# Last three query up tiles ahead of the last key up tiles, and no projection chunks beside the first two units of the latent attention

## Chip, cores and metric

One core of one Trainium2 chip. The metric is the device time of the whole kernel in microseconds, the median of several runs. Engines: PE is TensorE (matmul; PEld its weight loads), DVE is VectorE, ACT is ScalarE, POOL is GpSimd, SP is the sync engine, on whose queue nearly all loads are issued.

## What is computed

The reference runs two blocks of two layers each on 512 tokens of width 1024. The change lies in the first block, whose two layers have this token mixer (cut to what matters):

```
proj = h @ w_in[l]
qa, ka, va, iq, ik, iw, cq, ckv, kr, ga, gb = split(proj)
ya = dsa_attention(qa, ka, va, iq, ik, iw, positions, rel_bias)     # top-128 attention
q  = rms_norm(cq) @ w_uq        # 8 heads x (64 + 32 rotary)
kv = rms_norm(ckv) @ w_ukv      # 8 heads x (64 key + 64 value)
yb = mla_attention(q_nope, rope(q_rope), k_nope, rope(kr), v)       # latent attention
merged = sigmoid(ga) * (ya @ w_branch_a) + sigmoid(gb) * (yb @ w_branch_b)
```

After it come a layer norm, a convolutional feed-forward part and a second norm. The second block (retention, differential attention) isn't touched.

## The kernel before

**Weights.** They come in slots of 128 x 2048. SP loads a slot into one of two `w_raw` buffers, ACT rounds it to `w_hi` (line 1385, `split_hi`), POOL makes the remainder `w_lo` in four parts of 512 columns (line 583). After the fourth part the semaphore `w_ready` rises and PE may use the slot. A product of weights and activations is three matmuls (`mm3`, lines 718 to 720: high by high, low by high, high by low). A chunk is one `mm3` of 128 x 128 weights on 512 columns; a tile of a projection of h has 8 chunks.

**Up tiles.** In each layer the table `UPS` gives the order of the 12 up tiles of the latent attention: 8 query tiles ("q", h), two `mm3` each, from slot `SLOT_UQ`, and 4 key tiles ("k", j), one `mm3` each, from slot `SLOT_UKV`. From position 4 on, PE adds two columns of the modulation (line 748) behind each tile. A query tile is turned by DVE (lines 2170, 2171), summed by POOL (line 620) and copied by ACT to `qm` (line 1572). A key tile is copied by ACT in two halves to `km` (lines 1578, 1579). ACT goes through `UPS` in the same order. Right behind the copy of the last query tile, q7, it rounds the next slot, `SLOT_QK`, into the buffers which the query up weights have left:

```
if j == H - 1:
    split_hi(l, SLOT_UQ + 2)
```

Four value tiles follow on PE; the third and fourth wait for banks that hold the last two tiles of `UPS`. DVE copies them to `vm` (line 2176) once the last key copy is done. ACT then rounds slot `SLOT_QK + 1`.

**Latent attention.** `attention(l, 1)` on PE goes through 32 units (4 query blocks of 128 by 8 heads; a unit of block i has i + 1 key blocks). In step t it issues the scores of unit t (S, line 831), the transposes of unit t - 2 (T, line 844), which wait for that unit's exp, the products with v of unit t - 3 (line 855), and then the chunks that `BESIDE[1][t]` lists: the 64 chunks of the query and key projections of the other attention (`SLOT_QK` to `SLOT_QK + 3`, 8 tiles). The first chunk of a slot waits for `w_ready`. From unit 2 on S waits for the logits of two units before. DVE makes the logits and their maximum (line 1952), ACT the exp (line 1461), the copy of the transposes (line 1470) and the copy of a finished projection tile (line 1454), and behind every second tile the rounding of the slot after the next. The numbers of chunks a unit are a table written by hand, 3 for units 0 to 7, 2 for 8 to 23, 1 for 24 to 31.

Both layers run this with the same tables: layer 0 reaches it at about 178 us, layer 1 at about 1015 us.

Of the kernel before, what the change touches and what calls it, by code (L numbers as in the profile page):

```python
# [28 lines left out]
H = 8  # L29
# [79 lines left out]
def build(nc, a):  # L109
    ctx = ExitStack()  # L110
    with ctx:
# [309 lines left out]
        def beside(counts, steps):  # L421
            plan = []
            for c in counts:
                plan.append(steps[:c])
                steps = steps[c:]
            return plan
# [2 lines left out]
        NI = 2 * len(PAIRS)  # L429
        gate_steps = [(t, k) for t in range(KD) for k in range(KD)]  # L430
        BESIDE = [beside([3] * H + [2] * 2 * H + [1] * H, gate_steps),
                  beside([3] * H + [2] * 2 * H + [1] * H, gate_steps),
                  beside([5, 5, 6] * 4, gate_steps)]
        BESIDE.append([[(1 + s // KD, s % KD) for s in range(4 * u, 4 * u + 4)] for u in range(14)])
        BESIDE_TILE, BESIDE_LAST = (TILE_GB, TILE_QK, TILE_GA, TILE2_G2), (KD - 1, KD - 1, KD - 1, KD - 1)
# [1 line left out]
        def ended(kind, u):  # L437
            return next((t for t, k in BESIDE[kind][u] if k == BESIDE_LAST[kind]), None) if 0 <= u < len(BESIDE[kind]) else None

        UPS = [("q", 0), ("q", 1), ("q", 2), ("k", 0), ("q", 3), ("q", 4), ("k", 1), ("q", 5), ("q", 6), ("k", 2), ("q", 7),  # L440
               ("k", 3)]
        LOADS = 16 * 3
        BIAS_UNITS = [(i, 8 * i + q) for i in range(NB) for q in range(8)]
# [266 lines left out]
        def _(pe):  # L710
            def wait_slot(l, m):
                pe.wait_ge(w_ready, slot_no(l, m) + 1)

            def wait_bank(l, t, nbanks=4):
                pe.wait_ge(tile_evac, tdone(l, t - nbanks))
# [231 lines left out]
            for l in range(DEPTH):  # L947
# [51 lines left out]
                wait_slot(l, SLOT_UQ)  # L999
                for pos, (what, j) in enumerate(UPS):  # L1000
                    wait_bank(l, TILE_UQ + pos, 2 if pos < 2 else 4)
# [369 lines left out]
        def _(act):  # L1371
# [139 lines left out]
            for l in range(DEPTH):  # L1511
# [54 lines left out]
                act.wait_ge(kr_turned, l + 1)  # L1566
                for pos, (what, j) in enumerate(UPS):
                    b = banks[pos % 4]
# [245 lines left out]
        def _(dve):  # L1814
# [294 lines left out]
            for l in range(DEPTH):  # L2109
# [54 lines left out]
                for h in range(H):  # L2164
                    pos = UPS.index(("q", h))
                    b = banks[pos % 4]
# [390 lines left out]
```

## Time and profile before

| | |
|---|---|
| median of 3 runs | 2500.24 us (2500.0 to 2502.79) |
| profiled execution, its own time | 2498.26 us |
| its span | 2496.4 us |
| granted TensorE clock, mean | 0.986 |
| PE busy | 2405.9 us (96%) |
| DVE, ACT, POOL busy | 1205.1, 1006.0, 997.1 us |

The span runs from the first to the last instruction of one profiled execution. Times in rows are microseconds from the span's start. In a timeline a row begins with start and duration; x gives how many instructions are merged into it; what stands in brackets is how long the engine was idle before it and what released it. A matmul's duration reaches beyond the start of the next one, since matmuls are pipelined; the cadence is read from starts. PEclk is the granted clock of TensorE as a share of full speed, 2.4 GHz; 0.50 is its lower level, 1.2 GHz.

### The profile page before, as it was taken

The page shows a single profiled execution, that of the slowest core. Times are in us where ns is not written, and L with a number is a line of the kernel's source. Part 1 is how long each engine was busy: PE and PEld are TensorE (multiplying, and loading weights), DVE is VectorE, ACT ScalarE, POOL GpSimd, SP SyncE. Part 2 cuts the span into 40 slices and gives each one's busy share as a digit, 9 for nine tenths or more (in the row PEclk, how much of TensorE's full clock was granted, in tenths as well). Part 3 has the DMA queues.
Part 4 walks back from the last instruction along what each step waited for, and adds up shares of the span by engine and source line. Part 5 has one row for each costly group of instructions (what it writes and reads, how often), then busy time and mean ns, then how long its engine had stood idle before and what let it go on. Part 6 is the DMA issues. An engine that isn't in the chain of part 4 may idle for free.

```text
span 2496.4 us, 32249 instructions
## 1 busy us (share of the span) xinstructions
PE 2405.9 (96%) x11364; PEld 1889.9 (76%) x11364; DVE 1205.1 (48%) x2594; ACT 1006.0 (40%) x1677; POOL 997.1 (40%) x812
## 2 busy tenths in 40 slices
PE   7999999999999999999999999999999989999998
PEld 4778767778888876776677888887788867777756
DVE  7565665654344357567466343313340172244584
ACT  6444344344343244543433344423242353333463
POOL 3452222444444443413144444444444433444342
PEclk9999999999999999999999999999999999999999
DMA  8531134312226243212341222223222210222210
GB/s 334 216 112 67 45 108 148 123 68 101 99 75 238 93 187 135 80 44 88 128 152 68 97 88 101 82 99 108 84 85 84 101 73 34 84 85 85 85 43 35
DMA packets 52133, 259.68 MB, mean 104 GB/s; under 512 B 6385, under 2 KB 16369, under 8 KB 26417
## 3 DMA queue, kind: packets, MB, share of 16 engines
q1 hardware_dynamic: 50864, 249.76, 28.3%
q0 software_dynamic: 1152, 8.39, 0.8%
q8 instruction: 71, 1.16, 0.2%
q14 instruction: 46, 0.37, 0.0%
HBM read 249.61 MB, written 7.34 MB: 103 GB/s over the span
## 4 chain that ended last, share of the span: by engine, by line
PE 78%; issue 11%; POOL 4%; DVE 4%; ACT 2%; DMA 1%; DVEq 0%; POOLq 0%; SPq 0%; ACTq 0%
PE bank L718 21%; PE bank L720 21%; PE bank L719 21%; POOL w_lo L583 4%; PE bank L937 3%; PE bank L831 2%; PE bank L942 1%; PE bank L1197 1%; PE bank L855 1%; PE bank L1114 1%; PE bank L979 1%; PE bank L844 1%; PE bank L1186 1%; PE bank L1333 1%; DMA ada_early<-w_ada 0%
## 5 line engine op out<-in xcount | busy, mean ns | idle before, releaser
L583 POOL TENSOR_TENSOR w_lo<-w_raw,w_hi 128x512 fp32r<-128x512 f32 (+1 forms) x692 | 880.9, 1305 | 1304.5 <-ACT w_hi L1385 872.8
L718 PE MATMUL bank<-h_hi,w_hi 128*128 128x512 f32 x1616 | 658.8, 408 | 12.8 <-POOL w_lo L583 8.8
L720 PE MATMUL bank<-h_hi,w_lo 128*128 128x512 f32 x1616 | 632.5, 391 | 0.0
L719 PE MATMUL bank<-h_lo,w_hi 128*128 128x512 f32 x1616 | 631.0, 390 | 0.0
L718 PEld LDWEIGHTS bank<-h_hi,w_hi 128*128 128x128 f32 x1616 | 304.6, 188 | 92.7 <-issue 26.8
L720 PEld LDWEIGHTS bank<-h_hi,w_lo 128*128 128x128 f32 x1616 | 303.9, 188 | 65.5
L719 PEld LDWEIGHTS bank<-h_lo,w_hi 128*128 128x128 f32 x1616 | 304.6, 188 | 64.4 <-issue 7.0
L1385 ACT ACTIVATE w_hi<-w_raw 128x2048 fp32r<-128x2048 f32 (+1 forms) x114 | 201.4, 1766 | 291.0 <-PE bank L720 239.4
L2221 DVE SCALAR_TENSOR_TENSOR cv<-bank,par,cv 128x511 f32<-128x511 f32 (+1 forms) x176 | 131.6, 749 | 215.4 <-ACT cv L1627 201.0
L1627 ACT ACTIVATE cv<-bank,par 128x512 f32<-128x512 f32 x88 | 68.4, 779 | 235.4 <-PE bank L720 231.8
L1461 ACT ACTIVATE L<-L,nmax 128x128 f32<-128x128 f32 (+3 forms) x128 | 72.0, 563 | 191.7 <-DVE nmax L1952 191.3
L718 PE MATMUL bank<-u_hi,w_hi 128*128 128x512 f32 x352 | 138.0, 392 | 0.0
L720 PE MATMUL bank<-u_hi,w_lo 128*128 128x512 f32 x352 | 137.0, 389 | 0.0
L719 PE MATMUL bank<-u_lo,w_hi 128*128 128x512 f32 x352 | 137.0, 389 | 0.0
L1390 ACT ACTIVATE w_hi<-w_raw 128x2048 fp32r<-128x2048 f32 x68 | 129.7, 1908 | 0.0
L718 PE MATMUL bank<-w_hi,h_hi 128*128 128x512 f32 x256 | 101.5, 396 | 0.0
L720 PE MATMUL bank<-w_hi,h_lo 128*128 128x512 f32 x256 | 99.7, 390 | 0.0
L719 PE MATMUL bank<-w_lo,h_hi 128*128 128x512 f32 x256 | 99.7, 389 | 0.0
L2033 DVE SCALAR_TENSOR_TENSOR x<-bank,mod,x 128x512 f32<-128x512 f32 x32 | 24.0, 751 | 154.6 <-PE bank L720 137.2
L2270 DVE TENSOR_TENSOR rt<-bank,rope 128x512 f32<-128x512 f32 x32 | 22.1, 691 | 121.5 <-PE bank L1114 109.6
L718 PEld LDWEIGHTS bank<-u_hi,w_hi 128*128 128x128 f32 x352 | 66.1, 188 | 14.2 <-issue 0.5
L719 PEld LDWEIGHTS bank<-u_lo,w_hi 128*128 128x128 f32 x352 | 66.1, 188 | 14.1 <-issue 0.5
(392 smaller groups left out, 3923.0 us busy)
## 6 DMA issues: line engine op xcount, KB each, us to landing
w_raw<-w_stream SPq DMA_DIRECT2D x150, 1024.0 KB, 4.8
w_raw<-w_down SPq DMA_DIRECT2D x32, 704.0 KB, 4.0
ada_mid<-w_ada SPq DMA_DIRECT2D x20, 1024.0 KB, 5.0
ada_last<-w_ada SPq DMA_DIRECT2D x12, 1024.0 KB, 4.8
ada_early<-w_ada POOLq DMA_DIRECT2D x8, 1024.0 KB, 20.8
ada_late<-w_ada SPq DMA_DIRECT2D x8, 1024.0 KB, 6.7
bias_in<-bias_scratch SPq DMA_DIRECT2D x16, 256.0 KB, 3.0
bias_in<-bias_scratch SPq DMA_DIRECT2D x16, 192.0 KB, 2.7
```

Of the source, the lines that this page charges most:

```text
L583: ins = nc.gpsimd.tensor_tensor(w_lo[r][:, part], w_raw[r][:, part], w_hi[r][:, part].bitcast(fp32), ALU.subtract)
L718: nc.tensor.matmul(out, w[0][:, cols], xh, start=first, stop=False)
L719: nc.tensor.matmul(out, w[0][:, cols], xl, start=False, stop=False)
L720: return nc.tensor.matmul(out, w[1][:, cols], xh, start=False, stop=last)
L831: nc.tensor.matmul(banks[4 + t % 2][:, 0:n], q[rows, hh, i * P:(i + 1) * P], kk[rows, hh, 0:n], start=True, stop=True).then_inc(s_done, 1)
L844: ins = nc.tensor.transpose(banks[6 + u % 2][:, b * P:(b + 1) * P], L[u % 3][:, b * P:(b + 1) * P], ident)
L937: nc.tensor.matmul(banks[q][:, :], w[part][:, cols], xh[:, k, :], start=(k == 0 and part == 0), stop=False)
L1385: A_(w_hi[n % 2][:, 0:cols], w_raw[n % 2][:, 0:cols], ACT.Copy).then_inc(w_hi_done, 1)
L1390: A_(w_hi[n % 2][:, :], w_raw[n % 2][:, :], ACT.Copy).then_inc(w_hi_done, 1)
L1461: A_(L[t % 3][:, 0:n], L[t % 3][:, 0:n], ACT.Exp, bias=nmax[:, t:t + 1], scale=-1.0, accum_out=esum[:, t:t + 1]).then_inc(exp_done, 1)
L1627: A_(cv[s][c][:, :], banks[(t + c) % 4][:, :], ACT.Identity, bias=b, scale=w2).then_inc(conv_first, 1)
L2221: return V.scalar_tensor_tensor(out, banks[(t + c) % 4][:, 0:S - 2 + w], weight, out, ALU.mult, ALU.add)
```

## The change

It swaps two entries of `UPS`, so that q5, q6 and q7 follow each other ahead of k2 and k3, and rewrites the numbers of chunks beside the latent attention: none beside units 0 and 1, 4 beside units 2 to 7, as before from unit 8 on. Both for both layers.

```diff
-                  beside([3] * H + [2] * 2 * H + [1] * H, gate_steps),
+                  beside([0] * 2 + [4] * 6 + [2] * 2 * H + [1] * H, gate_steps),
...
-        UPS = [("q", 0), ("q", 1), ("q", 2), ("k", 0), ("q", 3), ("q", 4), ("k", 1), ("q", 5), ("q", 6), ("k", 2), ("q", 7),
+        UPS = [("q", 0), ("q", 1), ("q", 2), ("k", 0), ("q", 3), ("q", 4), ("k", 1), ("q", 5), ("q", 6), ("q", 7), ("k", 2),
                ("k", 3)]
```

What this makes of the order of instructions, first on ACT at the end of the up tiles. Before, from the last query copies (q5, q6) on; `w_hi_52` is the slot `SLOT_QK`, `w_hi_53` the one behind it:

```order
L1572 ACTIVATE qm<-bank 64x512 [waits q_rope,tile_done] x2
L1578 ACTIVATE km<-bank 64x512 [waits tile_done]
L1579 ACTIVATE km<-bank 64x512
L1572 ACTIVATE qm<-bank 64x512 [waits q_rope,tile_done]
L1385 ACTIVATE w_hi_52<-w_raw_50 128x2048 [waits w_full0]
L1578 ACTIVATE km<-bank 64x512 [waits tile_done]
L1579 ACTIVATE km<-bank 64x512
L1385 ACTIVATE w_hi_53<-w_raw_51 128x2048 [waits w_full1,tile_done]
L1461 ACT_TABLE_LOAD [waits logit]
```

And with the change:

```order
L1572 ACTIVATE qm<-bank 64x512 [waits q_rope,tile_done] x3
L1385 ACTIVATE w_hi_52<-w_raw_50 128x2048 [waits w_full0]
L1578 ACTIVATE km<-bank 64x512 [waits tile_done]
L1579 ACTIVATE km<-bank 64x512
L1578 ACTIVATE km<-bank 64x512 [waits tile_done]
L1579 ACTIVATE km<-bank 64x512
L1385 ACTIVATE w_hi_53<-w_raw_51 128x2048 [waits w_full1,tile_done]
L1461 ACT_TABLE_LOAD [waits logit]
```

The rounding of `SLOT_QK` now stands ahead of all four copies of k2 and k3 instead of between them.

On PE, at the start of the latent attention, from the last matmul of the value tiles on. Before:

```order
L720 MATMUL bank<-w_hi_53,c_lo 128x512
L831 MATMUL bank<-km,qm 128x128 [waits kr_stored,q_sum,idx_acc,tile_evac]
L718 MATMUL bank<-h_hi,w_hi_52 128x512 [waits tile_evac,w_ready]
L719 MATMUL bank<-h_lo,w_hi_52 128x512
L720 MATMUL bank<-h_hi,w_lo_54 128x512
L718 MATMUL bank<-h_hi,w_hi_52 128x512
L719 MATMUL bank<-h_lo,w_hi_52 128x512
L720 MATMUL bank<-h_hi,w_lo_54 128x512
L718 MATMUL bank<-h_hi,w_hi_52 128x512
L719 MATMUL bank<-h_lo,w_hi_52 128x512
L720 MATMUL bank<-h_hi,w_lo_54 128x512
L831 MATMUL bank<-km,qm 128x128 [waits q_sum]
```

And with the change:

```order
L720 MATMUL bank<-w_hi_53,c_lo 128x512
L831 MATMUL bank<-km,qm 128x128 [waits kr_stored,q_sum,idx_acc,tile_evac]
L831 MATMUL bank<-km,qm 128x128 [waits q_sum]
L831 MATMUL bank<-km,qm 128x128 [waits q_sum,logit]
L844 MATMUL bank<-ck,L_89 128x128 [waits ada_mod,tile_evac,exp_done]
L718 MATMUL bank<-h_hi,w_hi_52 128x512 [waits tile_evac,w_ready]
L719 MATMUL bank<-h_lo,w_hi_52 128x512
L720 MATMUL bank<-h_hi,w_lo_54 128x512
```

The scores of units 0, 1 and 2 and the transpose of unit 0 now stand between the value tiles and the first chunk; the six chunks that stood there follow behind. The instructions of DVE are in the same order as before.

## Rows read from the trace of the kernel before

**Rows 1.** The page: busy time by engine, chain that ended last, costliest group of lines.
```profile
PE 2405.9 (96%) x11364; PEld 1889.9 (76%) x11364; DVE 1205.1 (48%) x2594; ACT 1006.0 (40%) x1677; POOL 997.1 (40%) x812
...
PE 78%; issue 11%; POOL 4%; DVE 4%; ACT 2%; DMA 1%; DVEq 0%; POOLq 0%; SPq 0%; ACTq 0%
...
L718 PE MATMUL bank<-h_hi,w_hi 128*128 128x512 f32 x1616 | 658.8, 408 | 12.8 <-POOL w_lo L583 8.8
```

**Rows 2.** Timeline of PE, layer 1: start, us, engine, line, operation, [idle before <- releaser].
```profile
1006.15 0.49 PE L718 MATMUL bank<-c_hi,w_hi 128*128 128x512 f32 x1
...
1007.30 0.47 PE L718 MATMUL bank<-c_hi,w_hi 128*128 128x512 f32 x1
...
1014.00 0.50 PE L718 MATMUL bank<-w_hi,c_hi 128*128 128x512 f32 x1 [0.49 <-ACT km L1579]
...
1014.79 0.38 PE L831 MATMUL bank<-km,qm 96*128 96x128 f32 x2
1017.95 0.50 PE L718 MATMUL bank<-h_hi,w_hi 128*128 128x512 f32 x1 [2.77 <-POOL w_lo L583]
...
1018.60 0.63 PE L720 MATMUL bank<-h_hi,w_lo 128*128 128x512 f32 x1
...
1021.59 0.51 PE L831 MATMUL bank<-km,qm 96*128 96x128 f32 x2
...
1022.17 0.40 PE L719 MATMUL bank<-h_lo,w_hi 128*128 128x512 f32 x1
...
1024.03 0.39 PE L831 MATMUL bank<-km,qm 96*128 96x128 f32 x2
...
1024.28 0.48 PE L718 MATMUL bank<-h_hi,w_hi 128*128 128x512 f32 x1
```

**Rows 3.** Timeline of PE and of ACT, layer 0.
```profile
181.12 0.50 PE L718 MATMUL bank<-h_hi,w_hi 128*128 128x512 f32 x1 [2.77 <-POOL w_lo L583]
...
182.67 0.40 ACT L1461 ACTIVATE L<-L,nmax 128x128 f32<-128x128 f32 x1
```

**Rows 4.** Stretches: us, then PE, PEld, DVE, ACT, POOL busy (x), PEclk, DMA, GB/s.
```profile
182.00:186.00 4.00, 4.00 (x13) 3.23 (x12) 1.06 (x3) 1.65 (x5) 4.00 (x4) 0.57 0.75 262
506.00:513.00 7.00, 5.21 (x17) 4.17 (x18) 5.45 (x9) 3.77 (x5) 7.00 (x7) 0.53 0.00 0
1018.00:1022.00 4.00, 4.00 (x12) 3.17 (x13) 0.13 (x2) 1.78 (x3) 4.00 (x4) 0.57 0.78 262
1022.00:1106.00 84.00, 84.00 (x468) 68.39 (x468) 47.02 (x191) 40.83 (x105) 15.89 (x13) 1.00 0.15 51
```

**Rows 5.** Timeline of ACT (ScalarE), layer 1.
```profile
1010.46 0.59 ACT L1572 ACTIVATE qm<-bank 64x512 f32<-64x512 f32 x1 [1.30 <-DVE O L2171]
1010.96 1.90 ACT L1385 ACTIVATE w_hi<-w_raw 128x2048 fp32r<-128x2048 f32 x1
...
1013.35 0.59 ACT L1579 ACTIVATE km<-bank 64x512 f32<-64x512 f32 x1
...
1018.21 1.28 ACT L1461 ACT_TABLE_LOAD   x1 [1.30 <-DVE nmax L1952]
1019.50 0.40 ACT L1461 ACTIVATE L<-L,nmax 128x128 f32<-128x128 f32 x1
1019.81 0.18 ACT L1461 ACTIVATION_READ_ACCUMULATOR L<-L,nmax 128x1 f32 x1
```

**Rows 6.** Timeline of DVE (VectorE), layer 1.
```profile
1008.97 0.69 DVE L2170 TENSOR_TENSOR PT<-bank,rope 32x512 f32<-32x512 f32 x1 [1.59 <-PE bank L720]
1009.67 0.69 DVE L2171 TENSOR_TENSOR O<-bank,rope 32x512 f32<-32x512 f32 x1
1014.05 3.07 DVE L2176 COPY vm<-bank 128x512 f32<-128x512 f32 x4 [3.68 <-ACT km L1579]
...
1017.84 0.28 DVE L1952 CUSTOM_DVE_ANT_0 L<-bank,ck 128x128 f32<-128x128 f32 x1
```

**Rows 7.** Timeline of POOL (GpSimd), layer 1.
```profile
1012.93 9.91 POOL L583 TENSOR_TENSOR w_lo<-w_raw,w_hi 128x512 fp32r<-128x512 f32 x8 [1.21 <-ACT w_hi L1385]
```

## The prediction

> **What bounds the kernel now.** I read the busy shares first. TensorE (PE) is busy for 96% of the span and holds 78% of the chain that ended last [rows 1]; so what counts is where PE stands still. The groups by line say who stops it: before the first product of a weight slot it waited 12.8 us in all, 8.8 of them for GpSimd's low parts of the weights [rows 1]. The timeline of PE shows two of these waits at the place of the change. In layer 1 the scores of unit 0 start at 1014.79, and the first projection product follows at 1017.95, 2.77 us of it put down to the low parts [rows 2]; layer 0 does the same, with 2.77 us before 181.12 [rows 3]. So 5.5 of the 8.8 us are these two gaps. After them PE is never idle until the units run out: 84.00 us busy in the 84 from 1022 to 1106 [rows 4]. Hence one microsecond more or less of PE time ahead of this stretch is one microsecond at its end. I work in layer 1's times and take layer 0 as a copy: its exp starts 1.55 us after its first product [rows 3], as in layer 1 (1017.95 to 1019.50) [rows 2, 5].
>
> The gap costs more than its idle time. The granted clock over 1018 to 1022 is 0.57 of full speed, as it is over 182 to 186 [rows 4]: 4 x 0.43 = 1.72 us of clock are missing, which at the lower level of 1.2 GHz is a stretch of 3.4 us. The matmuls show it: seven take 1018.60 to 1021.59, 0.427 us each; eight from 1022.17 to 1024.03 take 0.233 each [rows 2]. A full 3.4 us at the low level thus does 54% of the work and costs 1.57 us, in each layer.
>
> **Part 1: q7 ahead of k2.** Key up tile 2 with its columns fills PE from 1006.15 to 1007.30 [rows 2], 1.15 us, and query tile 7 now goes in its place. VectorE took up q7 at 1008.97 when PE released it [rows 6], 1.67 us after the tile's start; it would now do so at 1007.82, by when it is free (it had stood idle for 1.59 us before 1008.97 [rows 6]). All that hangs on q7 moves 1.15 earlier. ScalarE's copy of q7 moves from 1010.46 to 1009.31, and the rounding of the first query/key slot (call it slot A) from 1010.96 to 1009.81 [rows 5]. GpSimd begins on A at 1012.93 and does 8 parts of two slots in 9.91 us [rows 7], so A's four take 4.96 and end at 1017.89, 0.06 before PE starts on it; now they end at 1016.74. **Slot A is ready 1.15 us earlier.**
>
> What is queued behind the moved rounding? The copies of k2 (two, formerly done before q7) and of k3. The last k copy began 2.39 us after the rounding did, at 1013.35, and lasts 0.59 [rows 5]. With two more copies of 0.59 between, it begins at 1009.81 + 2.39 + 1.18 = 1013.38: 0.03 later. Two wait for it: value tile 3 on PE, which started at 1014.00 after a 0.49 us stall [rows 2], and VectorE's four value copies, which started at 1014.05 [rows 6]. I take 0.04 us on each. Value tile 2 waits for k2 a little (until about 1012.9), which falls into the stall before tile 3 and costs nothing. No DMA is added; the load of the second-next slot is issued 1.15 earlier, on the sync queue only, and nobody is short of it.
>
> **Part 2: no chunks beside units 0 and 1.** The program of PE is now S0, S1, S2, T0, then chunks (S = scores, T = transpose of a unit). S2 waits for the logits of unit 0, and T0 for its exp. That chain isn't touched: VectorE's value copies from 1014.05, the modulation, the logits at 1017.84 [rows 6], ScalarE's table load at 1018.21, the exp at 1019.50, its sum at 1019.81 to 1019.99 [rows 5]. So S1 goes at 1015.2, S2 at 1018.2, T0 at 1020.06 and the first chunk at about 1020.20, though slot A has been ready since 1016.74. **The exp of unit 0 takes the place of the weights as what ends the gap, and the 1.15 us of part 1 buy nothing.** First chunk later: 1020.20 - 1017.95 = +2.25. What was behind it and now lies inside the gap: S2 with T0, 0.25 (a score and a transpose of one block take 1024.03 to 1024.28 [rows 2]), and S1, which I put at the same 0.25, its upper bound. That leaves +1.75 per layer.
>
> On the table load the Trainium skill differs ("ScalarE: Activation LUTs", What ACT_TABLE_LOAD costs): it puts a switch at 1.28 us and 1.38 more for a drain. By it T0 would come 1.38 later, and the sum would be 2.8 us higher. The trace agrees on the first part alone: the exp starts 1.29 us after the load [rows 5], and I take the row.
>
> **Part 3: the spread 4,4,4,4,4,4 for 3 x 8.** The chunk count stays 64: 24 up to unit 7 in both, the same after. Tile 1, whose end releases the rounding of the third slot, still ends beside unit 5. Tile 0 ends beside unit 3, not 2; its bank is wanted again at unit 6. A unit of one block now has 12 projection products instead of 9, so VectorE and ScalarE get more time for it, not less. Cost 0; cover gone would show as a PE wait beside units 2 to 7.
>
> **Part 4: the clock.** Not shown in this form, so bounded. PE works for only 0.4 us between 1015.2 and 1020.1. Low bound: the three small pieces keep the clock up, and the 1.57 us go: -1.57. Next: the low stretch stands where it stood (about 1018.4 to 1021.85) and hits work only from 1020.1; 1.8 x 0.46 = 0.81 instead of 1.57: -0.76. High bound: one more stretch of 3.4 us at the low level, as after the broken work near 506 to 513, where the clock is 0.53 over 7 us, 6.6 us at the low level [rows 4]: -0.76 + 1.57 = +0.81. The gap grows from 2.8 to nearly 5 us, so I lean to the high side: +0.25 per layer.
>
> **Sum.** Per layer 0.04 + 1.75 + 0.25 = 2.04; two layers +4.1 us. The profiled execution took 2498.26, which would give 2502.4. The median shown is 2500.24, so I forecast **2504.3**. What a measurement of this kernel can tell from no change is 0.2%, 5 us; so this is "the same", on the slow side.
>
> **Rivals.**
> *Slower: the clock stays low for a further stretch in both layers.* Place: PE after 1021.85, and after 185.6. Price: 0.81 instead of 0.25, so 2 x 2.60 = +5.2, 2505.4; a second further stretch in one layer makes it 2507.0. For it: the 506 to 513 row, and that the idle time is nearly twice what it was. Against: the clock came back after one stretch in both layers before. It decides if low clock is granted beyond about 1022 in layer 1 and 186 in layer 0. The Trainium skill speaks against this change here ("TensorE: Matmul & The Clock Gate", Why this matters for your kernels): idle gaps between bursts of matmuls are to be avoided, since they bring the lower clock. The trace agrees that the lower clock follows such a gap [rows 4]. Chance 0.27.
>
> *Faster: unit 0's exp is ready before slot A,* because something of VectorE's or ScalarE's chain moves forward with q7. Then chunks start at 1016.8 and the clock holds: -1.1 - 0.5 - 1.57, per layer -3.2, 2493.8. It decides only if the sum of unit 0 is there before 1016.74, 3.2 us earlier than now; yet VectorE's value copies hang on k3, which doesn't move. Chance 0.05.
>
> *Absorbed or halved:* the clock holds (-1.57 per layer: +0.4 in all, 2500.7), or a later wait with a clock of its own eats the delay. Against the latter: the waits behind the units are on ScalarE and VectorE work that PE itself releases. Chance 0.13.
>
> That the change doesn't do what it says is excluded by the order of instructions. The forecast keeps 0.55.
>
> **How the numbers follow.** Range: the forecast between the clock's ends (-0.76 and +0.81 per layer: 2502.3 to 2505.4), down to the clock that holds (2500.7) less half a microsecond of spread, up to a further stretch and spread: 2500.2 to 2507.3. Faster by over 0.2%: 0.05. Slower by over 5 us: the clock rival, 0.27. The same: the forecast and the absorbed case, 0.55 + 0.13 = 0.68.
>
> **What would show it.** Right: PE's waits at the first chunk no longer name the low parts; T0 is the first to wait after S2, released by ScalarE's exp; A's rounding starts about 1.15 earlier relative to S0; the first chunk is some 5.4 us behind S0 instead of 3.16; PE has no idle time up to the last unit. Wrong: T0 starts less than 4 us after S0, or PE waits beside units 3 to 8, or the clock stays at 1.00 through the gap.

## The result and the profile after

| | before | after |
|---|---|---|
| median | 2500.05 us (2498.63 to 2502.79, 9 runs) | 2508.71 us (2504.97 to 2509.68, 8 runs) |
| after / before | | 1.0032 [1.0023, 1.0042] |
| profiled execution, its own time | 2498.26 us | 2504.97 us |
| its span; granted clock | 2496.4 us; 0.986 | 2503.2 us; 0.984 |

One further run of the changed kernel (2733.08 us, granted clock 0.837) was disturbed and is left out of the comparison. The change costs 8.7 us, 0.32% [0.23, 0.42]: slower by more than 0.2%, above the top of the range (2507.3). The profiled execution is the fastest of the eight, so its rows show less of the loss than a usual execution has; two more profiles of the same program follow among the experiments.

The page of the changed kernel, same lines as [rows 1]:

```profile
PE 2410.4 (96%) x11364; PEld 1893.3 (76%) x11364; DVE 1206.4 (48%) x2594; ACT 1005.8 (40%) x1677; POOL 997.6 (40%) x812
...
PE 78%; issue 11%; POOL 4%; DVE 4%; ACT 2%; DMA 1%; DVEq 0%; SPq 0%; POOLq 0%; ACTq 0%
...
L718 PE MATMUL bank<-h_hi,w_hi 128*128 128x512 f32 x1616 | 659.3, 408 | 6.3 <-ACT gates_b L1456 3.3
```

The wait before the first product of a slot fell from 12.8 to 6.3 us, and GpSimd's low parts are no longer what ends most of it. Read alone this line looks like a gain of 6.5 us, and the shares of the chain have stayed as they were. But PE's busy time rose by 4.5 us with as many matmuls: some ran slower.

Timeline of PE after, layer 1 (start, us, engine, line, operation, [idle before <- releaser]), to be read beside [rows 2]:

```profile
1018.43 0.50 PE L718 MATMUL bank<-w_hi,c_hi 128*128 128x512 f32 x1 [0.26 <-ACT km L1579]
...
1019.23 0.61 PE L831 MATMUL bank<-km,qm 96*128 96x128 f32 x4
1022.96 0.80 PE L831 MATMUL bank<-km,qm 96*128 96x128 f32 x2 [3.12 <-DVE nmax L1952]
1024.82 0.48 PE L844 MATMUL bank<-ck,L 128*128 128x128 f32 x1 [1.07 <-ACT L L1461]
1024.95 0.78 PE L718 MATMUL bank<-h_hi,w_hi 128*128 128x512 f32 x1
...
1028.51 0.43 PE L720 MATMUL bank<-h_hi,w_lo 128*128 128x512 f32 x1
1028.78 0.40 PE L718 MATMUL bank<-h_hi,w_hi 128*128 128x512 f32 x1
```

S0 and S1 go together at 1019.23. S2 waits 3.12 us for the logits of unit 0, T0 another 1.07 for its exp, and the first chunk follows 5.72 us behind S0; before it was 3.16. The same in layer 0, timeline of PE:

```profile
184.03 0.49 PE L831 MATMUL bank<-km,qm 96*128 96x128 f32 x2 [3.12 <-DVE nmax L1952]
185.90 0.47 PE L844 MATMUL bank<-ck,L 128*128 128x128 f32 x1 [1.38 <-ACT L L1461]
```

Stretches of the changed kernel (us, then PE, PEld, DVE, ACT, POOL busy (x), PEclk, DMA, GB/s), beside [rows 4]:

```profile
1021.00:1025.00 4.00, 0.97 (x4) 0.68 (x4) 3.87 (x13) 2.35 (x6) 3.70 (x4) 0.59 0.67 229
...
1025.00:1029.00 4.00, 4.00 (x11) 3.16 (x12) 0.24 (x1) 0.82 (x5) 1.41 (x2) 0.55 0.40 131
1029.00:1113.00 84.00, 84.00 (x469) 68.48 (x468) 45.29 (x184) 40.09 (x100) 15.04 (x12) 1.00 0.13 46
```

In layer 1 the clock is at its lower level from 1021.8 to 1028.6, twice as long as before (in layer 0 from 185.5 to 188.9, as long as before). Its first three microseconds fall into idle time and cost little; the last 3.8 slow the first eight products behind the gap. Behind that, 84 us pass with no idle time and full clock, as before.

What ends the gap, on the other engines: ACT, then DVE, then POOL, timelines of layer 1 after.

```profile
1014.17 1.90 ACT L1385 ACTIVATE w_hi<-w_raw 128x2048 fp32r<-128x2048 f32 x1
...
1022.98 1.28 ACT L1461 ACT_TABLE_LOAD   x1 [1.64 <-DVE nmax L1952]
1024.28 0.40 ACT L1461 ACTIVATE L<-L,nmax 128x128 f32<-128x128 f32 x1
```

```profile
1018.48 3.07 DVE L2176 COPY vm<-bank 128x512 f32<-128x512 f32 x4 [4.90 <-ACT km L1579]
...
1021.79 0.91 DVE L1900 TENSOR_SCALAR mod<-mod 128x4 f32<-128x4 f32 x1
1022.62 0.28 DVE L1952 CUSTOM_DVE_ANT_0 L<-bank,ck 128x128 f32<-128x128 f32 x1
```

```profile
1016.15 4.97 POOL L583 TENSOR_TENSOR w_lo<-w_raw,w_hi 128x512 fp32r<-128x512 f32 x4 [1.21 <-ACT w_hi L1385]
1021.42 4.99 POOL L583 TENSOR_TENSOR w_lo<-w_raw,w_hi 128x512 fp32r<-128x512 f32 x4 [0.30 <-ACT w_hi L1385]
```

Slot A is ready at 1021.12, 1.9 us behind S0 instead of 3.1; nobody asks for it before 1024.95. The critical work in the gap is the four value copies, the modulation, the logits, the table load, the exp.

**Place and rest.** A stage is measured by the start of its first and of its last matmul. From S0 to S8 (the start of the scores of unit 8, by when both tables have issued 24 chunks) the first profile before took 24.85 us in layer 0 and 24.86 in layer 1; after takes 26.53 and 26.88: +1.68 and +2.02, **+3.7 us at the place of the change**. The sum forecast +4.1. The rest of the 8.7 us is elsewhere, where the order of instructions wasn't touched. That was the question for the experiments.

### The profile page after: what moved, and what is told of

The parts are those of the page before. It is cut to its first block, busy times and chain, and to the rows that moved or that the text cites. A ratio compares the mean times of both kernels' runs of the same rounds, so it can differ in the third digit from the quotient of the medians.

```text
span 2503.2 us, 32249 instructions
## 1 busy us (share of the span) xinstructions
PE 2410.4 (96%) x11364; PEld 1893.3 (76%) x11364; DVE 1206.4 (48%) x2594; ACT 1005.8 (40%) x1677; POOL 997.6 (40%) x812
## 4 chain that ended last, share of the span: by engine, by line
PE 78%; issue 11%; POOL 4%; DVE 4%; ACT 2%; DMA 1%; DVEq 0%; SPq 0%; POOLq 0%; ACTq 0%
PE bank L718 21%; PE bank L719 21%; PE bank L720 21%; POOL w_lo L583 4%; PE bank L937 3%; PE bank L831 2%; PE bank L942 1%; PE bank L1197 1%; PE bank L855 1%; PE bank L1114 1%; PE bank L979 1%; PE bank L844 1%; PE bank L1186 1%; PE bank L1333 1%; DMA ada_early<-w_ada 0%
## 5 line engine op out<-in xcount | busy, mean ns | idle before, releaser
L583 POOL TENSOR_TENSOR w_lo<-w_raw,w_hi 128x512 fp32r<-128x512 f32 (+1 forms) x692 | 881.4, 1306 | 1312.9 <-ACT w_hi L1385 881.3
```

What stands on the lines that cost most here:

```text
L583: ins = nc.gpsimd.tensor_tensor(w_lo[r][:, part], w_raw[r][:, part], w_hi[r][:, part].bitcast(fp32), ALU.subtract)
```

## The experiments

Ratios are against before, with a 95% interval. Edits are to the kernel before unless they say "the change +".

**e1: the change once more.**

> The changed kernel once more. In its first profile the first chunk of the latent attention came 5.7 us after the scores of unit 0 instead of 3.2, which shifts everything behind it by 3.6 to 4 us over both layers; the median of 9 runs was 8 us over before. Theory A (clock): the missing 4 us are further stretches at the lower TensorE clock behind the two longer gaps, in most executions though not in the profiled one: about +8 us again, and a profile with 4 us or more lost to the lower clock behind the gaps where the total is near 2508. Theory B (the first comparison caught an odd set of runs): about +4 us, 2504.

Measured 2508.11 us (7 runs) against 2499.97, ratio 1.0026 [1.0015, 1.0038]: +8.1. The size is no accident of one measurement: theory B falls. In this profile S0 to S8 takes 27.65 and 26.96 us: +4.9 at the place, and +11.2 over the whole span against the first profile before. So theory A, too, is right only in part: most of what is missing lies away from the gaps.

**e2: the new order of tiles alone.**

```diff
-        UPS = [..., ("k", 1), ("q", 5), ("q", 6), ("k", 2), ("q", 7),
+        UPS = [..., ("k", 1), ("q", 5), ("q", 6), ("q", 7), ("k", 2),
                ("k", 3)]
```

> Only the order of the up tiles, chunks beside units 0 and 1 as before. The first query/key slot is ready 1.15 us earlier and here PE waits for just that, so the gap behind the scores of unit 0 shrinks from 3.16 to about 2.0 us: -1.15 a layer, -2.3 in all. Theory A adds that a shorter gap brings the lower clock less often: -2.3 to -5.4 us, 2494.6 to 2497.7. Theory B: -2.3 us. A theory in which the later copies of k2 and k3 cost as much as the earlier slot gains: 0.

Measured 2495.10 us (11 runs), 0.9985 [0.9976, 0.9994]: -4.9. Timeline of PE, layer 1:

```profile
1012.41 0.39 PE L831 MATMUL bank<-km,qm 96*128 96x128 f32 x2
1014.36 0.50 PE L718 MATMUL bank<-h_hi,w_hi 128*128 128x512 f32 x1 [1.56 <-POOL w_lo L583]
...
1015.16 0.39 PE L718 MATMUL bank<-h_hi,w_hi 128*128 128x512 f32 x1
```

The gap has shrunk from 2.77 to 1.56 us by the 1.2 of slot A, and the products behind it run at 0.23 us each: no lower clock in either layer's gap. S0 to S8 is 22.03 us, 2.8 shorter in each layer: 1.2 of wait and 1.6 of clock. One half of the change, taken alone, is a gain.

**e3: the new numbers of chunks alone.**

```diff
-                  beside([3] * H + [2] * 2 * H + [1] * H, gate_steps),
+                  beside([0] * 2 + [4] * 6 + [2] * 2 * H + [1] * H, gate_steps),
```

> Only the chunk counts (none beside units 0 and 1), up tiles in the old order. The first chunk waits for the exp of unit 0, which comes at 1020.0 in layer 1 in any case, after the slot (1017.9 in the old order). So all of the loss is here and this kernel is as slow as the change: +8 us under theory A, +4 under B. If the swap itself costs something: less than the change by that much.

Measured 2504.46 us (11 runs), 1.0020 [1.0011, 1.0029]: +4.5. S0 to S8 takes 26.27 and 26.79 us: +3.4 at the place, where the change's first profile has +3.7. So the loss at the place is this part's. In the median, though, this kernel isn't as slow as the change, as theory A wanted: it is 3.7 us below e1, which was measured beside it. At the place 0.7 of that is accounted for: in the old order S2 waits 2.79 us for the logits where the change has 3.12, and the difference is one small instruction of DVE, here

```profile
1020.88 0.58 DVE L1900 TENSOR_SCALAR mod<-mod 128x4 f32<-128x4 f32 x1
```

against 0.91 above. The other 3 us this run leaves open; the intervals of the two kernels overlap.

**e4: the change + matmuls that fill the gaps.** Twelve behind S1, seven behind S2, on operands that lie ready; nothing reads their result.

```diff
+            def keep_busy(count):
+                for j in range(count):
+                    nc.tensor.matmul(banks[6][:, :], h_hi[:, j % 4, 0:P], h_hi[:, j % KD, :], start=True, stop=True)
...
+                    if kind == 1 and t in (1, 2):
+                        keep_busy({1: 12, 2: 7}[t])
```

> The change, with 12 more matmuls of 512 columns (results unused) behind the scores of unit 1 and 7 behind those of unit 2, in both layers: they fill most of the idle time without moving the waits, so that the clock stays up. What is left is the bare lateness of the first chunk, about +1.8 us a layer, less the 1.57 us a layer which the lower clock cost before: +0.4 us in all under theory A, 2500.5, and no stretch under clock 1.00 near 185 and 1022 us. If the 8 us are not the clock's: +4 or more.

Measured 2500.97 us (11 runs), 1.0004 [0.9995, 1.0013]: +1.0. Timeline of PE, layer 1 (L810 are the added matmuls, L835 the scores, L850 the transposes):

```profile
1016.61 0.61 PE L835 MATMUL bank<-km,qm 96*128 96x128 f32 x4
1016.97 2.98 PE L810 MATMUL bank<-h_hi 128*128 128x512 f32 x12
1020.37 0.49 PE L835 MATMUL bank<-km,qm 96*128 96x128 f32 x2 [0.42 <-DVE nmax L1958]
1020.61 1.85 PE L810 MATMUL bank<-h_hi 128*128 128x512 f32 x7
1022.30 0.27 PE L850 MATMUL bank<-ck,L 128*128 128x128 f32 x1
```

The first chunk comes at 1022.34, 5.73 us behind S0 as in the change, but the clock stays at its upper level, and S0 to S8 falls to 25.23 and 25.17: 1.3 and 1.7 less than in the change's first profile. Against before 0.7 is left at the place. With the clock put right the loss is 7 us smaller than in e1, more than the 3.0 to 4.2 that it returns at the place. The Trainium skill ("TensorE: Matmul & The Clock Gate", Why this matters for your kernels) asks that long idle gaps between bursts of matmuls be avoided, since they bring the lower clock; by that rule the gap's clock is what is to be mended. The trace agrees: with the gaps filled, no lower clock is granted between S0 and S8 in either layer.

**e5: the change + the exp table loaded early.** ACT does a one-column exp behind the rounding of the second slot, so that the table is there when the logits come.

```diff
+                A_(small[:, 16:17], ck[:, C_ONE:C_ONE + 1], ACT.Exp)
```

> The change, with one exp of a single column (its result unused) on ScalarE behind the rounding of the second query/key slot, so that the table load of 1.28 us lies before the logits and not between them and the exp of unit 0. Theory C (the exp of unit 0 is what ends the gap in the changed kernel): T0 and the first chunk come 1.28 us earlier in each layer, the first chunk about 4.4 us behind the scores of unit 0 instead of 5.7: -2.6 us against the change, and up to 1.57 a layer more where the shorter gap saves a low stretch, so 2502.5 to 2505.5. Rival D (the chain up to the logits, VectorE, is the only bound and ScalarE's part is hidden): no difference, 2508.

Measured 2501.66 us (11 runs) against 2499.09, 1.0009 [1.0000, 1.0018]: +2.6, a little below the 2502.5 to 2505.5 of theory C and far from the 2508 of rival D. Timeline of ACT, layer 1:

```profile
1022.06 1.28 ACT L1582 ACT_TABLE_LOAD   x1
...
1023.70 0.40 ACT L1461 ACTIVATE L<-L,nmax 128x128 f32<-128x128 f32 x1
```

T0 no longer waits, the first chunk is 4.44 us behind S0 (1019.93 to 1024.37) instead of 5.72, and S0 to S8 takes 25.46 and 25.23: 1.1 and 1.7 less than after. The 1.28 us by which the chunk came forward are the load's duration. So the load's 1.28 us stood on the path that ends the gap, as the sum had it. The drain of 1.38 us that the Trainium skill adds ("ScalarE: Activation LUTs", What ACT_TABLE_LOAD costs) isn't seen: the exp of the change starts 1.30 us after its load, and here the one-column exp 1.29 after.

**e6: before + eleven matmuls behind S0**, the same `keep_busy`, with nothing else changed.

> The kernel before, with 11 more matmuls of 512 columns (results unused) behind the scores of unit 0, which fill 2.6 of the 2.8 us gap in each layer. The waits stay where they are. If each gap costs one stretch of 3.4 us at the lower clock: -1.57 a layer, -3.1 in all, 2496.9, and no low stretch near 182 and 1018 us. If the lower clock behind the gaps comes from something else: 0. If the clock's price is larger than its own stretch (a shift of later stalls): more than -3.1.

Measured 2497.07 us (11 runs), 0.9992 [0.9983, 1.0001]: -2.0. S0 to S8 is 23.29 and 23.30, 1.56 less in each layer: the price of one stretch of lower clock, as the prediction had it. Of these 3.1 us at the place 2.0 show in the median, whose interval (-4.2 to +0.2 us) holds the 3.1 and just holds nothing.

**e7: the new order, no chunks beside unit 0 only.**

```diff
+                  beside([0] + [4] * 3 + [3] * 4 + [2] * 2 * H + [1] * H, gate_steps),
```

> Tiles in the new order, no chunks beside unit 0 only (then 4, 4, 4, 3, 3, 3, 3). The first chunk then stands behind the scores of unit 1 and ahead of the transpose of unit 0, and waits for the slot, as in the kernel with the new order of tiles alone (2495.1); the scores of unit 1 move into the gap, 0.25 us a layer: 2494.6. If it is the leaving out of chunks as such that costs, and not the wait for the exp, it would lie between that and the change: about 2500.

Measured 2495.82 us (11 runs), 0.9990 [0.9981, 0.9999]: -3.3, where 2494.6 was expected and 2500 would have spoken for the chunks as such. PE's wait for the low parts in the gap is 1.34 us, with 0.44 more for the exp of unit 0, ahead of T0. Chunks beside unit 1 are enough to keep most of the wait for the exp out of the gap.

**e8: all key tiles but the first last, old numbers of chunks.**

```diff
-        UPS = [..., ("k", 0), ("q", 3), ("q", 4), ("k", 1), ("q", 5), ("q", 6), ("k", 2), ("q", 7),
-               ("k", 3)]
+        UPS = [..., ("k", 0), ("q", 3), ("q", 4), ("q", 5), ("q", 6), ("q", 7), ("k", 1), ("k", 2),
+               ("k", 3)]
```

> Old chunk counts, and key up tile 1 moved behind the query tiles as well (q3, q4, q5, q6, q7, k1, k2, k3). The rounding of the first query/key slot comes another key tile (1.15 us) earlier, so the gap shrinks from 1.8 to about 0.6 us. Six copies of key tiles then stand behind the rounding, which end when the four did. Expected: another -1.15 a layer, 2492.8. If VectorE can't keep the pace of five query tiles in a row (1.4 of 1.8 us), or a value tile waits longer for its bank: 2495 or more.

Measured 2494.66 us (12 runs), 0.9980 [0.9971, 0.9988]: -4.4. The gap shrank by 0.28 us more than in e2 and not by 1.15; the expectation's own caveat, a value tile's bank, is what happened. Timeline of PE, layer 1:

```profile
1014.12 0.47 PE L718 MATMUL bank<-h_hi,w_hi 128*128 128x512 f32 x1 [1.28 <-DVE vm L2176]
```

The weights no longer end the gap; the first chunk now waits for the bank of a value tile. By the median e2 and e8 can't be told apart (2495.10 and 2494.66), and either is faster than the kernel before and the changed one.

**e9 and e10: before + 9 or 18 matmuls ahead of T4 in both layers.** PE is busy there on both sides, so this adds work and nothing else (results unused again): it asks what some microseconds at this place cost at the end.

```diff
+                        if kind == 1 and t == 6:
+                            keep_busy(9)
```

> The kernel before, with 9 more matmuls of 512 columns (results unused) ahead of the transposes of unit 4 in each layer: 9 x 0.23 = 2.1 us of busy PE a layer, no idle time and no clock of its own. It makes everything behind as late as the change does at its own place (+3.7 and +4.9 us in two profiles), though the change measured +8.1 and +8.7. Theory E (later stalls meet the clock otherwise when they come 2 to 4 us later, and more of them bring low stretches): as for the change, +6 to +8 us, 2506 to 2508. Theory F (the rest lies behind the change's own gaps, in executions that were not profiled): +4.2 us and no more, 2503.6.

> The same with 18 matmuls, 4.2 us of busy PE a layer. Theory F: +8.3 us. Theory E: not in line with the run before: the added time above 8.3 us comes or goes in steps of 1.6 us a stall, so +8.3 give or take 3.

9 matmuls a layer are 4.2 us in all, 18 are 8.3. e9 measured 2507.68 us (8 runs) against 2499.75, 1.0030 [1.0019, 1.0041]: **+7.9**. e10 measured 2508.82 (9 runs), 1.0030 [1.0020, 1.0040]: +9.1. So 4.2 us cost nearly twice themselves, and 8.3 little more than themselves. Theory F, that what is lost at the place comes out one for one, wanted 2503.6; all eight runs of e9 lie above it (2505.16 and more), but the interval of the difference, 4.7 to 10.2 us, begins close to it. What speaks against F more strongly is where the profiles and the clock put the time, below. e10 lies within what both theories allow (8.3, and 8.3 give or take 3). A surcharge of e9's size for every shift doesn't fit it; a smaller one of about 1 us isn't excluded.

**e11 and e12: before and the change once more**, for a second look at before and a third at the change.

> The kernel before itself: a second profile, to see in which stages its low clock stretches lie. In the first, the stages from 850 to 900 us and from 0 to 100 us held one or two fewer than in 8 of 9 profiles of its variants, so part of the 4 us may be that profile's luck: I expect the stage from 850 to 870 us 1.6 us longer than in the first profile, and the median as it was, 2500 (no more than 1 us off).

> The change itself for a third profile: the two gaps with 3.7 to 5 us more than before in all. Theory F wants more stretches there in an average execution, so 5 us or more; theory E wants them in the stages behind (300 to 480, 496 to 525, 850 to 870 us). Median about 2508.

e11: 2498.86 us (10 runs), 0.9993 [0.9984, 1.0003]. e12: 2506.39 (10 runs), 1.0024 [1.0015, 1.0033], +6.6. The median of e11 is as expected, its profile isn't: the stretch from 850 to 870 us, expected 1.6 us longer, is as long as in the first, so the first profile wasn't lucky there. The profiles, cut at the same matmuls and set against the first profile of before, in us (the start-up, where nothing differs between these programs, moves by up to 3 by itself):

| | start to 100 | gap, layer 0 | 300 to 480 | 496 to 525 | 850 to 900 | gap, layer 1 | whole |
|---|---|---|---|---|---|---|---|
| before again (e11) | +2.9 | +0.8 | 0 | 0 | 0 | 0 | +3.9 |
| after | +2.1 | +1.7 | 0 | 0 | +0.4 | +2.0 | +6.7 |
| change again (e1) | +0.7 | +2.8 | +1.6 | +1.5 | +2.0 | +2.1 | +11.2 |
| change, third (e12) | -0.6 | +2.8 | +1.5 | +1.5 | +2.0 | +2.1 | +9.9 |
| 4.2 us of work (e9) | +2.8 | +2.9 | +1.6 | 0 | +0.4 | +1.9 | +10.6 |
| 8.3 us of work (e10) | -0.7 | +4.1 | 0 | +1.4 | +2.0 | +3.9 | +12.7 |

The whole span was cut into 30 stages; those not listed agree to 0.2 us, but for 0.7 in e9 (1334 to 1361) and 1.6 in e10 (1230 to 1250). What moves is for the most part a matter of 1.5 or 1.6 us, the price of one stretch of lower clock. Added up behind 300 us and without layer 1's gap, the change's three profiles lose 0.4, 5.1 and 5.0 us there, e9 2.7 and e10 5.0, and the second profile of before nothing. In four of these five, then, theory E holds: the time lies in stages behind, in which the program wasn't altered. The rows show it, first where the first attention of layer 0 ends (L855, L864), timeline of PE before and then of e12:

```profile
399.86 1.10 PE L855 MATMUL bank<-va,PT 128*128 128x64 f32 x8 [0.87 <-ACT PT L1470]
401.41 0.66 PE L864 MATMUL bank<-ck,O 128*128 128x128 f32 x4 [0.45 <-DVE O L1972]
401.82 0.47 PE L718 MATMUL bank<-yb_hi,w_hi 128*128 128x512 f32 x1
402.14 0.39 PE L719 MATMUL bank<-yb_lo,w_hi 128*128 128x512 f32 x1
```

```profile
402.28 1.10 PE L855 MATMUL bank<-va,PT 128*128 128x64 f32 x8 [0.87 <-ACT PT L1470]
403.84 1.12 PE L864 MATMUL bank<-ck,O 128*128 128x128 f32 x4 [0.45 <-DVE O L1972]
404.61 0.78 PE L718 MATMUL bank<-yb_hi,w_hi 128*128 128x512 f32 x1
405.18 0.63 PE L719 MATMUL bank<-yb_lo,w_hi 128*128 128x512 f32 x1
```

The waits are the same to the hundredth, 0.87 and 0.45 us; only the clock granted behind them isn't. The stretches of 8 us from there, and of 12 us ahead of layer 0's last norm where PE has no idle time, first before, then e12:

```profile
399.60:407.60 8.00, 7.29 (x37) 6.16 (x38) 1.60 (x4) 5.61 (x10) 4.79 (x4) 1.00 0.64 241
858.00:870.00 12.00, 12.00 (x69) 10.17 (x69) 3.28 (x9) 3.35 (x4) 3.84 (x4) 1.00 0.23 89
```

```profile
402.00:410.00 8.00, 7.27 (x31) 6.12 (x32) 1.46 (x3) 5.15 (x9) 4.78 (x4) 0.79 0.65 253
860.00:872.00 12.00, 12.00 (x56) 10.35 (x55) 4.70 (x11) 3.04 (x4) 3.47 (x3) 0.72 0.50 176
```

One part of these 12 us is unlike the rest: 32 matmuls of one column each. Timeline of PE, e12:

```profile
861.59 4.14 PE L756 MATMUL bank<-ck,ada_acc_late 128*128 128x1 f32 x32
```

The lower clock comes at 864.5, towards their end. Both profiles of before have the same 32 matmuls and keep the upper level.

That this isn't a whim of single profiles is borne out by the clock granted in every timed execution. From its mean, the time at the lower level is (1 - clock) x 2 x time, an estimate, since the clock is given to three places: 74 to 76 us in the three sets of runs of before (29, 35 and 28 runs), 85 to 87 in the three of the change (8, 7 and 10 runs), 85 in e9, 83 in e3, 80 in e5, but 76 in e10 (whose profiled execution has 85 and is its slowest) and 70 to 73 in e2, e4, e6, e7 and e8. Some 11.5 us more in the change than in before, of which its three profiles show 3.4, 6.8 and 6.8 (more than before's) between S0 and S8 of the two layers; about 6 lie elsewhere, and at 0.46 us each they cost 2.7 if all of it hits work. (Where elsewhere this mean can't say, and the start-up is part of it.) In e9 it is 9 us more, 3.4 of them in these stretches: 5.6 elsewhere, 2.6 us, close to the 3.1 that its median has beyond what lies at the place (4.8).

The kernels that became faster pay as well. From the first profile of before to theirs, e2, e6, e7 and e8 gained 5.6, 3.1, 4.8 and 6.3 us between S0 and S8; their medians gained 4.9, 2.0, 3.3 and 4.4. They have no lower clock in either gap, 6.8 us less of it than before, yet by their runs only 1 to 3 us less in all: the rest turns up elsewhere. All twelve profiles of other kernels than before are at least 0.4 us longer behind 300 us (again without layer 1's gap); the two of before agree to 0.1 us. A part of the surcharge may thus be that the kernel before happens to lie well; no run tests that.

**The balance.** Between S0 and S8 the change's three profiles lost 3.7, 4.9 and 4.9 us, on average 4.5. The medians lost 8.7, 8.1 and 6.6. Two to four microseconds more are lost elsewhere; in two of the three profiles it is clock lost at later stalls that the program didn't alter, 5 us of it, and in the third 0.4. Against the second profile of before the place costs 0.8 less. What stays open: which stage pays how often in a usual execution, for there is one profile to a program run; and why a shift of 4 us meets the clock worse than one of 8.

## Why the prediction was wrong

**Part 1 held.** A's rounding starts 5.06 us ahead of S0 instead of 3.83: 1.23 earlier, forecast 1.15. It bought nothing in the change, as said, and e2 shows what it buys when the exp isn't in the way. The up tiles ahead of S0 take 0.1 us longer (forecast 0.04). "No DMA is added" and nobody was short of a slot. One thing I passed over: the second slot's low parts now start at 1021.42, while before GpSimd went through eight parts without a break [rows 7], and beside that start DVE's L1900 takes 0.91 us instead of 0.57. It stands in the very chain that ends the gap, and was 0.34 us longer in each layer.

**Part 2 held in kind and nearly in size.** The first chunk is 5.72 us behind S0, forecast 5.41; the missing 0.31 is L1900. The step "+1.75 a layer" can be set free of the clock: where the low stretch hits work for 2.9 us (layer 0 of after) or 3.8 us (layer 1) instead of 3.4, at 0.46 each, the differences of 1.68 and 2.02 leave 1.9 and 1.8. Forecast with part 1: 1.79. The table load was priced right (e5). The chain by which "the exp of unit 0 takes the place of the weights" is in the rows.

**Part 3 held.** No wait of PE beside units 2 to 8.

**Part 4 was right at the place on average, too narrow in its reach.** Forecast +0.25 a layer, bounds -0.76 and +0.81. Measured in the same way: -0.2 and +0.2 in after. In e12, where layer 0 got two stretches (181.9 to 188.7), 5.4 us of them hit work and cost 2.5 instead of 1.6: +0.9. But layer 0 of e11, the kernel before, also got two (182.6 to 189.5) and lost 0.8. The number of stretches that a gap gets isn't a property of the gap. The rival "the clock stays low for a further stretch" was true of layer 1 in all three profiles of the change, at a price of 0.2 and not 0.8, since the stretch begins 3 us ahead of the first chunk and nearly half of it is spent idle. In e1 and e12 it was true of layer 0 too, at its full price of 0.9. Its sum, +5.2 at the place, is closer to the 4.9 of these two than the forecast's 4.1, and its 2505.4 to 2507.0 came nearest of all cases to the medians, if for a reason that covers only the place.

**The sum at the place was right: +4.1 forecast, 3.7 to 4.9 measured.** That its clock term came out on average is partly luck, as it was a lean between bounds, and layer 0 alone varied from -0.2 to +0.9. What failed is the step that turned it into a time: "one microsecond more or less of PE time ahead of this stretch is one microsecond at its end". It is, at the end of that stretch; I read on as if it held to the end of the kernel. Under *Absorbed or halved* I asked only whether a later wait could eat the delay, and took "a later wait with a clock of its own" as something that could only shorten it. The opposite happened: where the profiles show it, later stalls kept their length (0.87 and 0.45 us near 400 us) and were met by more of the lower clock. e9 prices this without the change in it: 4.2 us of plain work cost 7.9. With that term (+2 to +4) the forecast would have been 2506.3 to 2508.3, and a range upward from there would have held the result. Its rows stood in view: the profile before has some 72 us at the lower level in thirteen places, against 6.8 at the two gaps that I priced.

The rival *Faster* had no part in it, since the value copies wait for k3 as it said against itself.

## What to carry to other kernels

When a wait on one resource hides another that ends only little later, moving the work away from it turns a gap with one cause into a longer one with another: give the earlier slot to work that can use it (e2: -4.9 us), and leave the cover where it is. A local sum priced from a trace was good to half a microsecond a layer here, but on a kernel with many short stalls a shift of a few microseconds also changes which of them get the lower clock; add that as a term with a width of its own (here from nearly nothing to 4 us), and measure it with plain added work before a small difference is put down to the edit.

## What the runs showed of the hardware

- The lower clock came in stretches of 3.4 us or two or three of them in a row, and the same program with the same waits gets it in different places: 71.7 us in one profile of before, 81.9 in another. It doesn't follow each stall of PE: behind the same 0.87 and 0.45 us of waiting near 400 us it came in three of the fourteen profiles (e1, e12, e9) and stayed away in eleven. Nor is its start tied to the gap: in layer 0 it came 4.2 us behind S0 in one profile of before and 1.6 us in the other (S0 at 177.96 and 181.03, the clock falls at 182.17 and 182.64).
- It can also begin where the profile shows no idle time of PE: at 864.5 us in e12, during 32 matmuls of one column each. Behind the same 32 it didn't come in either profile of before.
- Plain matmuls in the gaps held the clock at its upper level (e4, e6), and gaps of 1.6 us (e2) left it there where 2.8 us (before) did not, in both layers.
- A DVE instruction on 128 x 4 elements (L1900) took 0.56 to 0.62 us or 0.91 to 0.95, the longer in the eight profiles in which GpSimd had begun a new row of L583 about 0.4 us before (0.91 after, 0.94 in e2 and e4), the shorter in the six in which such a row was long under way (0.57 before, 0.58 in e3). That was seen, not tested.
